# Weighing the values one step later in three software-pipelined attentions

## What is computed

```python
# first block, layers 0 and 1: 4 pairs of differential heads, 8 forgetting heads
p = jax.nn.softmax(logits, axis=-1)
p = p[:, :, 0] - lam * p[:, :, 1]                 # differential heads
oa = rms_norm(einsum(p, va), diff_sub_g) * (1 - lam_init)
ob = einsum(jax.nn.softmax(logits + decay), vb)   # forgetting heads
x = x + rms_norm(concat(oa, ob) @ w_out, attn_post_g)
# second block: three masked attentions over the same queries, gated and added
out = g0 * o_compressed + g1 * o_selected + g2 * o_window
mixed = sigmoid(merge_0) * (y_mlstm @ w_branch_0) + sigmoid(merge_1) * (out @ w_branch_1)
h = h + mixed @ w_out
```

## Time and profile before

| what | us |
| --- | --- |
| timed runs, median of 3 (lowest to highest) | 2111.53 (2109.34 to 2111.93) |
| the profiled execution, its own time | 2109.28 |
| its span, first to last instruction | 2107.9 |
| TensorE busy in the span | 2053.5 (97%) |
| attention loop of L0, L1, M, about | 97 to 251, 723 to 878, 1498 to 1640 |

### The profile page before, as it was taken

The page is one execution under the profiler, slowest core; times in us unless marked ns, Lnnn a source line. Parts: engine busy times, 40 slices in busy tenths (PEclk is TensorE's granted clock), DMA queues, the critical chain, the costliest instruction groups (busy, mean ns, idle before and its releaser), DMA issues.

```text
span 2107.9 us, 25685 instructions
## 1 busy us (share of the span) xinstructions
PE 2053.5 (97%) x10399; PEld 1665.8 (79%) x10399; DVE 1047.4 (50%) x1890; ACT 808.2 (38%) x1533; POOL 257.3 (12%) x330
## 2 busy tenths in 40 slices
PE   7999999999999999999999999999999999999998
PEld 7867788888888767788888888888766788888887
DVE  6474454324437475454334446746566445433443
ACT  5255452222224355452222235344456333322322
POOL 3124410000001114210000000000366000000000
PEclk9999999999999999999999999999999999999999
DMA  5433333333223322233333232422321324323331
GB/s 167 113 72 78 98 100 99 97 95 100 91 95 95 95 62 71 70 106 96 94 100 99 87 95 63 110 60 80 86 61 33 93 80 126 99 90 102 98 95 65
DMA packets 271674, 190.69 MB, mean 90 GB/s; under 512 B 19740, under 2 KB 241108, under 8 KB 271556
## 3 DMA queue, kind: packets, MB, share of 16 engines
q1 hardware_dynamic: 264080, 174.28, 28.3%
q0 software_dynamic: 7328, 14.72, 3.0%
q10 hardware_dynamic: 148, 0.04, 0.0%
HBM read 183.72 MB, written 4.24 MB: 89 GB/s over the span
## 4 chain that ended last, share of the span: by engine, by line
PE 86%; DVE 7%; ACT 4%; issue 1%; POOL 1%; DMA 1%; DVEq 0%; ACTq 0%; POOLq 0%
PE bank L635 50%; PE bank L681 8%; PE bank L683 8%; PE bank L682 8%; PE bank L781 3%; PE bank L748 2%; PE bank L767 2%; DVE weights_hi_lo L1041 1%; DVE arena L1475 1%; ACT weights_hi_lo L1753 1%; DVE x_residual L1195 1%; PE bank L866 1%; ACT arena L1812 1%; PE bank L868 1%; PE bank L867 1%
## 5 line engine op out<-in xcount | busy, mean ns | idle before, releaser
L635 PE MATMUL bank<-h_features,weights_hi_lo 128*128 128x512 f32 (+1 forms) x5112 | 1114.4, 378 | 8.2 <-DVE weights_hi_lo L1041 6.8
L635 PEld LDWEIGHTS bank<-h_features,weights_hi_lo 128*128 128x128 f32 x5112 | 917.6, 189 | 189.2 <-DVE weights_hi_lo L1041 8.9
L1041 DVE TENSOR_TENSOR weights_hi_lo<-weights,weights_hi_lo 128x1024 fp32r<-128x1024 f32 (+2 forms) x337 | 395.6, 1179 | 489.8 <-ACT weights_hi_lo L1753 489.3
L1753 ACT ACTIVATE weights_hi_lo<-weights 128x1024 fp32r<-128x1024 f32 (+2 forms) x337 | 337.7, 1007 | 273.4 <-PE bank L683 247.9
L681 PE MATMUL bank<-weights_hi_lo,hidden 128*128 128x512 f32 x528 | 205.9, 390 | 0.0
L683 PE MATMUL bank<-weights_hi_lo,hidden 128*128 128x512 f32 x528 | 205.4, 389 | 0.0
L682 PE MATMUL bank<-weights_hi_lo,hidden 128*128 128x512 f32 x528 | 205.4, 389 | 0.0
L1869 ACT ACTIVATE arena<-arena 128x512 f32<-128x512 f32 x66 | 41.7, 632 | 270.2 <-DVE arena L1205 270.2
L2245 POOL TENSOR_SCALAR arena<-arena,row_stats 128x256 f32<-128x256 f32 (+5 forms) x140 | 127.3, 921 | 139.7 <-DVE row_stats L1125 63.7
L1205 DVE TENSOR_TENSOR arena<-bank,arena 128x512 f32<-128x512 f32 x66 | 69.5, 1054 | 118.8 <-PE bank L635 109.1
L1872 ACT ACTIVATE hidden<-arena 128x512 fp32r<-128x512 f32 x66 | 41.7, 632 | 217.9 <-DVE arena L1211 217.9
(11 more groups left out here) (363 smaller groups left out, 2071.6 us busy)
## 6 DMA issues: line engine op xcount, KB each, us to landing
weights<-in_w_in_dram SPq DMA_DIRECT2D x78, 512.0 KB, 4.0
weights<-in_w_gate_dram SPq DMA_DIRECT2D x66, 512.0 KB, 3.8
weights<-in_w_up_dram SPq DMA_DIRECT2D x66, 512.0 KB, 3.8
weights<-in_w_down_dram SPq DMA_DIRECT2D x60, 512.0 KB, 3.6
weights<-in_w_out_dram SPq DMA_DIRECT2D x24, 512.0 KB, 3.7
bias_rows<-decay_scratch POOLq DMA_DIRECT2D x16, 256.0 KB, 4.3
weights<-in_w_in_dram SPq DMA_DIRECT2D x13, 256.0 KB, 3.3
weights<-in_w_down_dram SPq DMA_DIRECT2D x12, 256.0 KB, 2.6
```

Of the source, the lines that this page charges most:

```text
L635: last = e.matmul(out_ap, l, r, start=(j == 0), stop=(j == len(pairs) - 1))
L1041: e.tensor_tensor(pair_view(i, 1), raw_view(i), pair_view(i, 0).bitcast(F32), ALU.subtract).then_inc(done, tick(("split", i)))
L1753: e.activation(pair_view(i, 0), raw_view(i), ACT.Copy).then_inc(done, tick(("hi", i)))
```

## The change

The product with the values moves from iteration i = k+4 to k+5 for the group that ends with step k. What takes the values out of their bank moves along (VectorE from k+5 to k+6, ScalarE's high part from k+4 to k+5). The four uses of `HEAD_AT` move by one iteration, so the head norm's GpSimd, TensorE, ScalarE and VectorE parts go from 4h+9, +10, +11, +12 to 4h+10, +11, +12, +13; what writes the normed head (`HEAD_OUT_AT`, 4h+22) stays. The loops run one iteration longer, and M's two late gates go from 47 and 49 to 51 and 53.

```diff
-LAG = 6
-HEAD_AT = {4 * h + 10: h for h in range(N_DIFF)}
+LAG = 7
+HEAD_AT = {4 * h + 11: h for h in range(N_DIFF)}
...
-LATE_GATE_AT = {47: 0, 49: 1}
+LATE_GATE_AT = {51: 0, 53: 1}
...
-                        if i - 4 in groups:
-                            weigh_values(groups[i - 4])
+                        if i - 5 in groups:
+                            weigh_values(groups[i - 5])
...
-                        if i - 5 in groups and groups[i - 5].final:
-                            g = groups[i - 5]
+                        if i - 6 in groups and groups[i - 6].final:
+                            g = groups[i - 6]
...
-                        if i - 4 in groups and groups[i - 4].final:
-                            g = groups[i - 4]
+                        if i - 5 in groups and groups[i - 5].final:
+                            g = groups[i - 5]
```

## The result

Median 2123.95 us (2121.54 to 2126.07, 4 runs) against 2110.61 (2109.34 to 2111.93, 4 runs): ratio 1.0063, 95% interval 1.005 to 1.0076. The change costs 13.3 us, the forecast was 6.6 and a range up to 2123. A second series of the same kernel gave 1.0062 (1.0049 to 1.0075). The profiled execution of the kernel after took 2121.54 us with a span of 2120.2, 12.3 over the span before.

A forecast was written before the change was run, and what follows sets the result against it. TensorE was taken as the bound (86% of the chain). L0 1.4, L1 4.5 and M 0.7 gave +6.6 on 2109.28, 2115.9; with 2.25 for the runs' median, 2118.0 us. Own range 2115.5 to 2121, whole 2110 to 2123.

The forecast's parts named there:

- over 2.5: Iteration 12 in L1: the product would wait over 2.5 us, ended by VectorE's emptying of the bank (L1157).
- M's middle: M before its end: -0.7 us each at turns 14, 26, 38, +0.8 and about +0.5 elsewhere; -0.8, bounds -3 and +2.4.
- L0, +1.4 forecast: L0's attention: +1.1 us up to the tile of 13, +0.7 behind the tiles, -0.4 at the end.
- the 0.79 of iteration 5: L0's iteration 5: a wait of 0.79 us taken to vanish, already counted in the +1.1 before the tile of 13.
- L1, +4.5 forecast: L1's attention: +1.0 us up to the tile of 13, +3.9 behind the tiles, -0.4 at the end.
- my 1.0: L1 up to the tile of 13: the middle between +0.2 us if the clock stays up and +1.7 if it falls.
- 3.9: L1 behind the tiles, 13 to 27: product waits for VectorE's late emptying of the bank, +3.9 us, bounds 0 and 6.
- my 1.2: L1 behind the tile of 27: a wait of 1.2 us, since L1365 starts 0.9 us late there.
- M's end, +1.5 forecast: End of M: the turn of 47 waits for GpSimd, branch tile at 1641.1, not 1639.64; +1.5 us, bounds 0 and +3.
- rival (3): The clock falls at each wait over 2.5 us in L0, L1 and M, 1.5 us each: +11, 2122.5 us; chance 0.07.
- (1): Bank waits find cover, as VectorE is earlier in odd iterations of both layers: +1.5, 2113.0 us; chance 0.30.
- (2): Waits vanish: L1827's copies and the bank are early, M gains, its end costs nothing; iteration 12 decides; 2104.5 us, chance 0.10.

The follow-up runs named there:

- e10: Kernel after, with unused filling matmuls in TensorE's waits in L0, L1 and M, order of banks kept: median 2118.5 us, ratio 1.0034 to before.
- e2: Kernel after with the layers' part undone, so only M changed (later values, gates at 51 and 53): median 2118.2 us, ratio 1.0038 to before.
- e3: Kernel before with the loop one iteration longer and only M's late gates moved, to 51 and 53: median 2110.9 us, ratio 1.0001.
- e4: Kernel before with only M's values moved later, its gates still at 47 and 49: median 2114.5 us, ratio 1.0016.
- e14: Kernel before with L1's query and key tiles taken out of PSUM by ScalarE, per-token factors left out: 2111.9 us, one run.
- e5: Kernel after with two banks for the weighted values and six, not seven, for other attention steps: median 2118.8 us, ratio 1.0037 to before.
- e9: Kernel after, unchanged, run again for a second profile and more runs: median 2123.62 us.
- e15: Kernel after with L1's query and key tiles taken out of PSUM by ScalarE, per-token factors left out: 2117.8 us, one run.
- e12: M's values later, gates at 47 and 49, plus filling matmuls in both layers' iteration 11 and M's waits, banks kept: median 2109.9 us, ratio 0.9997 to before.

## Why the prediction was wrong

**The direction and the mechanism of the layers were right.** L1827's waits went; the bank's wait came in their place, in even iterations (2.48 and 2.47 us before the product of 12, for my "over 2.5"); slower was given 0.6. Two steps failed: the clock, and M's middle.

**L0, +1.4 forecast, +1.3 measured.** Iteration 12 as worked out (143.8 against 143.5). Not foreseen: the turn in iteration 6 waits 1.5 us for L1146. I had set the 0.79 of iteration 5 as "vanished"; TensorE came to VectorE's mixing earlier and waited there. And the product of iteration 10 waits 1.90 us, where that of 9 waited 1.01.

**L1, +4.5 forecast, +5.3 measured.** For the stretch to the tile of 13 I gave 1.0, and it is 1.1 (773.62 less 725.27, against 772.07 less 724.81). That is luck in part: my 1.0 was the middle between a fall of the clock behind the product of 12 and none. None came there (1.78 us for the product), but one came behind the wait in iteration 6, and the product of 12 starts 45.9 us behind the scores of step 3, where it is 44.4 in L0. Behind it 3.9 became 4.8 to the first output tile, 3.7 of it idle; the 1.0 of longer busy time was not in my sum. The waits behind the tiles of 13 and 17 were 1.05 and 0.79 for my 0.9 each; those behind 15, 21 and 25 are missing, and behind 27 my 1.2 is there with 1.09, but as a wait of the scores for the queries and keys of L1365 (three such, 1.5 us in all). I had counted what TensorE does behind the tile as cover, and not that the product itself had been the cover of L1365.

**M's middle, -0.8 forecast, +0.6 measured.** This step failed in its sign. I took 0.7 off three times, for the turns of 14, 26 and 38 that wait for GpSimd. In 26 the wait is gone. In 14 and 38 GpSimd is no longer waited for, and the turn waits 0.91 us for VectorE's copy L1139 instead (and the one before it 0.34 and 0.36 for ScalarE's); in 22 and 46 the wait for L1111 rose from 0.49 and 0.43 to 0.91. The rows of 14 and 46:

```profile
1539.85 0.63 PE L767 MATMUL bank<-shape_consts,token_scratch 128*128 128x128 f32 x4 [0.91 <-DVE arena L1139]
...
1626.16 0.63 PE L767 MATMUL bank<-shape_consts,token_scratch 128*128 128x128 f32 x4 [0.91 <-DVE row_stats L1111]
```

What was late next was not asked for there.

**M's end, +1.5 forecast, +3.3 measured.** The schedule part was right: 1.8 with the clock up (e10: 23.0 us from the scores of step 47 to the branch tile, before 21.2), though the one wait of 2 to 3 us came as four of 0.7 to 1.0. The other 1.5 is the clock.

**The clock is the term that was mis-sized.** I asked only whether one known fall, at 769, would come again, and put the case of more falls aside as rival (3), with 0.07 and 2122.5. It is what happened in size, though not in place: no stall of 2.5 us brought it each time, but the sum of many. The runs give 2.5 to 5.0 us (at most 16.3 less 11.3 lost), and filling the waits took 5.1 us off the median; my sum had 0 for it outside L1. The schedule's part, 8 to 10.4 by the runs and 9.0 by the profiles (1.3, 5.3, 2.4), stood against 6.6; of the gap of 2.4 M's middle is 1.4 and L1 0.8.

**The other rivals.** (1), that the waits find cover, fell: L1's waits behind 13 are there. (2) fell at the iteration it named: VectorE's copy there ends 2.4 us behind TensorE's last work.

## What to carry to other kernels

When an operation is moved by one iteration, its buffer's emptying moves with it: ask on which side of the long tile both now stand, and what the emptying engine does right behind that tile. Ask too what the moved operation itself had been covering. When TensorE is the bound, price a new wait of it twice, as time and as clock, and take the clock from many runs (time against granted clock), since a single profile shows chance falls. Take such a split as a range: time against clock, run by run, gave less for each 0.001 than the product of time and clock does. And cheap matmuls in an unavoidable wait can give the clock's share back (5.1 us here, in e10), if they disturb neither the order of banks nor the work behind.

## What the chip showed that I had not expected

**The same wait, two clocks.** Up to M, the kernels e2, e3, e4 and before run the same instructions. Behind the same wait in iteration 11 of L0 the clock fell in e2 and not in e3 (e2's row first; e3's product is the second):

```profile
141.75 2.38 PE L781 MATMUL bank<-token_scratch,arena 128*128 128x256 f32 x8 [2.38 <-DVE token_scratch L1157]
```

```profile
142.33 1.78 PE L781 MATMUL bank<-token_scratch,arena 128*128 128x256 f32 x8 [2.38 <-DVE token_scratch L1157]
```

It fell there in e2, e4 and e14 (product 2.38, 2.21 and 2.82 us) and not in before and e3 (1.78). In all five exactly one of the two layers' iteration 11 has the fall, and the three with it in L0 are the three with one near 1445. So the falls of one run hang together: it matters when a wait comes, not only how long it is. The Trainium skill (page "TensorE: Matmul & The Clock Gate", Part 1 on the HAM clock gate) says that the monitor runs freely and does not start anew with a kernel, so that the same kernel can differ from run to run; these traces agree. The section "A second HAM failure mode: psum-queue depth-cycling" of the same page of the Trainium skill says that frequent short idles between groups of matmuls make the clock go down and up as well; the traces agree at M's end, where the clock fell behind four waits of 0.67 to 0.99 us with turns between them.

**Short waits in a row.** No single wait at M's end is over 1 us, and the clock fell behind them in each of the five profiles that have them without filling (after, e2, e5, e9, e15).

**What stays open.** Why M's later values alone (e4) lose up to 4.6 us more to the clock than e3 is not shown wait by wait: its profile has falls at 1503 to 1510 and 1605 to 1612, the second behind waits of 0.36 and 0.91 us, and filling some of M's waits and iteration 11 (e12) took the loss from 15.8 to 9.6. How much of that belongs to M was not tried alone.
